# A hybrid decoder step on one core: k is projected first, q and k are turned inside v's projection, and the last stage issues all its gathers at once

## What is computed

```python
q_a = _rmsnorm(q_a.reshape(shp), q_norm_g[:, None, :])
k_a = _rmsnorm(k_a.reshape(shp), k_norm_g[:, None, :])
s = jnp.einsum('bnqrhe,bnkrhe->bnrhqk', qb, kk) * (E ** -0.5)
```

## Time and profile before

| | |
|---|---|
| median of three runs | 3180.73 us (3177.16 to 3184.13) |
| the profiled execution, its own time | 3173.9 us |
| its span, first to last instruction | 3172.2 us |
| attention stage, about 32 to 798 us | PE busy 96% from 32 to 790 us |
| combine stage, about 3120 us to the end | PE idle, DMA engines busy 69% from 3119 to 3172 us |

### The profile page before, as it was taken

The page is one execution under the profiler, slowest core; times in us unless marked ns, Lnnn a source line. Parts: engine busy times, 40 slices in busy tenths (PEclk is TensorE's granted clock), DMA queues, the critical chain, the costliest instruction groups (busy, mean ns, idle before and its releaser), DMA issues. The chain is left out here.

```text
span 3172.2 us, 33419 instructions
## 1 busy us (share of the span) xinstructions
PE 2852.2 (90%) x12984; PEld 1945.6 (61%) x12984; DVE 897.1 (28%) x1773; ACT 625.5 (20%) x1392; POOL 528.3 (17%) x543
## 2 busy tenths in 40 slices
PE   7999999999379999999999987999999499999992
PEld 4555776776157777777777776888855244444441
DVE  3222222222614334333433432212112411111113
ACT  2111112112013233332322332112000011111110
POOL 3122122222223122222312210000000000000002
PEclk9999999999669999999999969999999699999996
DMA  6002000200701011101100135662031399999994
GB/s 218 11 8 97 14 24 14 74 31 30 250 1 27 1 28 28 28 1 28 28 1 28 28 130 170 207 212 88 21 110 54 146 412 392 382 382 382 386 371 173
DMA packets 161553, 397.80 MB, mean 125 GB/s; under 512 B 10651, under 2 KB 102043, under 8 KB 149087
## 3 DMA queue, kind: packets, MB, share of 16 engines
q1 hardware_dynamic: 151662, 361.58, 31.2%
q0 software_dynamic: 6176, 21.83, 2.0%
q10 hardware_dynamic: 3584, 12.58, 1.0%
HBM read 323.01 MB, written 73.14 MB: 125 GB/s over the span
## 5 line engine op out<-in xcount | busy, mean ns | idle before, releaser
L440 PE MATMUL at_p<-ring,hT 128*128 128x512 f32 x1152 | 532.1, 610 | 1.6 <-PEq L2663 1.6
L981 PE MATMUL dn_p<-hT,ring 128*128 128x344 f32 x1536 | 483.7, 460 | 14.4 <-DVE dn_nq L1376 12.0
L440 PEld LDWEIGHTS at_p<-ring,hT 128*128 128x128 f32 x1152 | 304.2, 273 | 161.1 <-issue 80.8
L981 PEld LDWEIGHTS dn_p<-hT,ring 128*128 128x128 f32 x1536 | 282.3, 193 | 137.2 <-DVE dn_nq L1376 13.5
L1857 PE MATMUL mx_prod<-hT,ring 128*128 128x256 f32 (+1 forms) x1024 | 233.2, 381 | 3.0 <-PEq L2663 3.0
L1857 PEld LDWEIGHTS mx_prod<-hT,ring 128*128 128x128 f32 x1024 | 194.4, 190 | 31.1 <-issue 3.1
L2569 DVE TENSOR_TENSOR ex_hid<-ex_ps_u,ex_gated 128x512 f32<-128x512 f32 (+1 forms) x32 | 22.2, 693 | 507.5 <-PE ex_ps_u L2504 272.8
L1551 POOL TENSOR_TENSOR ring<-ring,dn_level 128x512 f32<-128x512 f32 x96 | 127.1, 1343 | 148.2 <-DVE ring L1395 80.3
L566 DVE COPY oBT<-at_p 128x256 f32<-128x256 f32 (+1 forms) x96 | 52.5, 547 | 299.6 <-PE at_p L490 299.5
L1533 POOL TENSOR_SCALAR ring<-ring,conv_w 128x1024 f32<-128x1024 f32 x24 | 72.0, 2998 | 363.0 <-ACT ring L1200 363.0
L1857 PE MATMUL mx_prod<-oBT,ring 128*128 128x256 f32 (+1 forms) x512 | 118.4, 385 | 12.0 <-DMA ring<-in_w_out_b 12.0
(11 more groups left out here) (427 smaller groups left out, 3953.9 us busy)
## 6 DMA issues: line engine op xcount, KB each, us to landing
ring<-in_w_e_gate SPq DMA_DIRECT2D x32, 2048.0 KB, 12.0
ring<-in_w_e_up SPq DMA_DIRECT2D x32, 2048.0 KB, 15.5
ring<-in_w_e_down SPq DMA_DIRECT2D x32, 2048.0 KB, 14.2
y_scratch<-tails SPq DMA_DIRECT2D x16, 2048.0 KB, 8.2
ring<-in_w_in SPq DMA_DIRECT2D x13, 2048.0 KB, 13.5
ring<-in_w_in SPq DMA_DIRECT2D x32, 512.0 KB, 6.6
ring<-in_cache_swa_kv SPq DMA_DIRECT2D x6, 2048.0 KB, 13.6
mx_w_a<-in_w_out_a SPq DMA_DIRECT2D x32, 256.0 KB, 2.9
```

Of the source, the lines that this page charges most:

```text
L440: mm = nc.tensor.matmul(bank, perm_tokens(m.hT, g, t, k), weights[:, k, :], start=(k == 0), stop=(k == KD - 1))
L981: mm = nc.tensor.matmul(bankp[j][:, 0:C3], weights[:, k, WPOS[part], :], m.hT[:, k, j * C3:(j + 1) * C3], start=(k == 0), stop=(k == KD - 1))
```

## The change

In the attention the projections go k, q, v, and v shares k's bank (`pv = pk`). `turn_qk` is split: `turn_k` stands after the 18th of the 24 matmuls, `turn_q` after the 22nd, and the last two matmuls and weigh 3 stand behind it. q is turned into a bank of its own, `tq`. q's weight is no longer multiplied in by POOL for prompt tiles: q is turned as it comes from the scaling (`sq`), where its weight belongs to a partition, and the copy to `qT` multiplies by the column `q_column` and by 1/8. ACT loads `q_column` with six small DMAs at the start of the stage. On DVE and ACT the steps for k and q change places, and the copy of kT stands before the scaling of q. The wait for v's copy moves from the scores to weigh 0. In the combine every tile has its own place in `ring`, POOL issues its 18 gathers without a wait, and the additions go in place into the residual `x1`, which is stored.

```diff
-                    for w, (name, bank) in enumerate((("q", pq), ("k", pk), ("v", pv))):
-                        if n >= 1 and name == "k":
-                            pe.wait_ge(S["k_scaled"], n)
+                    for name, bank in (("k", pk), ("q", pq), ("v", pv)):
+                        if n >= 1 and name == "q":
+                            pe.wait_ge(S["q_scaled"], n)
                         if name == "v":
-                            pe.wait_ge(S["q_scaled"], n + 1)
+                            pe.wait_ge(S["k_scaled"], n + 1)
...
-                def turn_qk(n):
+                def turn_k(n):
                     a = number[jobs[n]]
...
+                    pe.wait_ge(S["k_normed"], n + 1)
+                    if a >= 1:
+                        pe.wait_ge(S["probs_ready"], 8 * a)
...
+                def turn_q(n):
+                    pe.wait_ge(S["q_scaled"], n + 1)
+                    for hp in range(4):
+                        mm = nc.tensor.transpose(tq[:, hp * P:(hp + 1) * P], sq[:, 0, hp * P:(hp + 1) * P], m.ident)
+                    mm.then_inc(S["q_turned"], 1)
...
                         turn_probs(a, 2)
-                        fill(source, 5)
+                    else:
+                        fill(source, 18 if turns else 24)
+                    if turns:
+                        turn_k(jobs.index(nxt))
+                        fill(source, 4)
+                    if att:
                         weigh_values(a, 2)
                         turn_probs(a, 3)
-                        fill(source, 1)
+                    if turns:
+                        turn_q(jobs.index(nxt))
+                        fill(source, 2)
+                    if att:
                         weigh_values(a, 3)
-                    fill(source, 24)
-                    if nxt in number:
-                        turn_qk(jobs.index(nxt))
...
+                        if b == 0:
+                            dve.wait_ge(S["gain_landed"], 16 * 2 * NG)
+                        nc.vector.tensor_scalar(qT, tq.rearrange("p (h k) -> p h k", h=4),
+                                                m.q_column[:, nxt[0]:nxt[0] + 1], float(E) ** -0.5, ALU.mult, ALU.mult
+                                                ).then_inc(S["qT_ready"], 1)
...
+                for g in range(NG):
+                    for r in (0, E):
+                        act.dma_start(m.q_column[r:r + E, g:g + 1],
+                                      m.q_gain[:, g, :].rearrange("a (e c) -> (a e) c", c=1)).then_inc(S["gain_landed"], 16)
...
+                        if which == "q" and t < NT:
+                            continue
                         pool.wait_ge(S[which + "_scaled"], n + 1)
...
-                    if t >= 2:
-                        pool.wait_ge(both_added, t - 1)
                     for i in range(2):
-                        nc.gpsimd.indirect_dma_start(y[0:r, t % 2, i, :], None, m.y_scr,
+                    nc.gpsimd.indirect_dma_start(y[t][i][0:r], None, m.y_scr,
...
```

More of the change, by code:

```diff
@@ L526, in _ @@
                         pe.wait_ge(S["kT_ready"], a + 1)
-                        pe.wait_ge(S["v_copied"], jobs.index(att) + 1)
                         scores(a, 0)
                         scores(a, 1)
-                        fill(source, 24 if nxt and nxt[1] == NT else 6)
+                        fill(source, 6 if turns else 24)
                         turn_probs(a, 0)
@@ L622, in square @@
                     act.wait_ge(S[which + "_projected"], n + 1)
-                    if n >= 1:
-                        act.wait_ge(S[which + "_normed"], n)
+                    if which == "k" and n >= 1:
+                        act.wait_ge(S["k_normed"], n)
+                    elif n >= 1 and jobs[n - 1] in number:
+                        act.wait_ge(S["q_turned"], number[jobs[n - 1]] + 1)
+                    elif n >= 1:
+                        act.wait_ge(S["q_normed"], jobs[n - 1][0] + 1)
                     nc.scalar.activation(sq[banded(t, w), w, :], bank[banded(t, w), :], ACT.Square
@@ L669, in _ @@
                     r = rows(t)
-                    for w, which in enumerate("qk"):
+                    for which in "kq":
+                        w = "qk".index(which)
                         own = stat[banded(t, w), w]
@@ new lines, in stage_combine, with _ @@
+    rows = m.ring.rearrange("p a b -> p (a b)")
+    y = [[rows[:, (2 * t + i) * D:(2 * t + i + 1) * D] for i in range(2)] for t in range(NT + 1)]
+    first_added, both_added, stored = (semaphore(nc, m, "cb_" + n) for n in ("first_added", "both_added", "stored"))
+    y_landed = [semaphore(nc, m, f"cb_y_landed{t}") for t in range(NT + 1)]
+    with nc.Block() as block:
+        @block.gpsimd
+        def _(pool):
+            for t, r in TILES:
+                for i in range(2):
+                    nc.gpsimd.indirect_dma_start(y[t][i][0:r], None, m.y_scr,
+                                                 bass.IndirectOffsetOnAxis(m.dest_u[0:r, i, t:t + 1], 0)
+                                                 ).then_inc(y_landed[t], 16)
+        @block.vector
+        def _(dve):
+            for t, r in TILES:
+                x1 = m.x1[t][0:r]
+                dve.wait_ge(y_landed[t], 32)
+                nc.vector.scalar_tensor_tensor(x1, y[t][0][0:r], m.row_w[0:r, 0, t:t + 1], x1, ALU.mult, ALU.add
+                                               ).then_inc(first_added, 1)
+                dve.wait_ge(first_added, t + 1)
+                nc.vector.scalar_tensor_tensor(x1, y[t][1][0:r], m.row_w[0:r, 1, t:t + 1], x1, ALU.mult, ALU.add
+                                               ).then_inc(both_added, 1)
+        @block.sync
+        def _(sp):
+            for t, r in TILES:
+                sp.wait_ge(both_added, t + 1)
+                dst = m.y_prompt[t * P:(t + 1) * P, :] if t < NT else m.y_sample
+                sp.dma_start(dst, m.x1[t][0:r]).then_inc(stored, 16)
+            sp.wait_ge(stored, 16 * (NT + 1))
```

93 lines of the change are left out of this document (26 added, 67 removed).

## The result

The changed kernel takes 3140.43 us (median of four executions, 3138.79 to 3146.40), the kernel before beside it 3179.75 us; the ratio is 0.9878, with a 95% interval from 0.9861 to 0.9896. That is 39 us or 1.2% less, where 29.5 us were forecast. Executions of one kernel differ by up to 14 us here, and much of that lies in stages that the change does not touch (from the last weigh of the attention to the first gather of the combine they take 2323.0 us in some traces and up to 2335.1 in others), so what follows compares stage by stage.

The account below looks back on a forecast made before the run. PE, idle before each attention step's scores, and the DMA engines in the combine were taken as bounds. Attention -26, start +3.5, combine -7 sum to -29.5; from the median 3180.7 that gives 3151 us (chance 0.55), range 3140 to 3164.

Parts of the forecast that it names:

- The seams: Attention: 24 waits before a step's scores vanish, 1.14 us each, 27.4 less 1.4 for broken matmul rows: -26 us.
- The cover it worked out for qT's copy: Attention: transposes, two matmuls and weigh 3 give 2.56 us where 1.45 is needed, 1.1 us more.
- the low end of 0.69 to 1.38: Attention: assumed length in us of the new two-factor copy to qT; 0.69 taken, twice that the high end.
- The start: Start of attention: the first projection now needs k's chunk, which is loaded second and lands at 35.8 us: +3.5 us, once.
- The combine: Combine: gathers no longer wait for additions, so the eighth tile lands at 3157.0 us and the end is 3165.3: -7 us.
- I take 350: 28.0 us: Combine: 9.8 MB left after 3129 us flow at 350 GB/s, chosen between 336 and 367, taking 28.0 us.
- the rival in which stores give way to gathers: Combine: gathers go ahead of stores, so it gains 11 us instead of 7; 3147 us, chance 0.10.
- The additions do hold up issues: Combine rival: ten gather issues each wait for an addition of 1.28 us; gain 4 us instead of 7; 3154 us, chance 0.18.
- Half the seams: Attention rival: qT's two-factor copy takes 2.4 us, scores wait 0.6 per seam, 14 us of gain lost; 3165 us, chance 0.11.
- the waiting turn_q: Attention rival: q's chain 4 us longer, PE waits 2.7 us for q's scaling in 24 steps; 3216 us; slower, chance 0.06.
- the 1.3 us of slack: Attention: PE has 6.4 us of work from the 16th matmul to turn_q, against 5.1 until q's scaling ends.
- the allowance for scatter and for the share of stores: Lower end of the range: 3147 less 3.5 us scatter, 1.4 for the seam's upper end, 2 for unknown stores' share: 3140.

Follow-up runs that it names:

- the three copies: Changed kernel with three more copies of the turned q on VectorE ahead of the one to qT; first projection to last weigh 750.1 us, 12.0 more.
- The attention alone: Attention part of the change with the combine of the kernel before; 3158.24 us, ratio 0.9932.
- two tiles ahead: Changed kernel in which a tile's gathers wait for the additions of the tile two before; combine 58.4 us against 40.5.
- the run with one input: Changed kernel with the combine's 18 additions each replaced by a sum over one gathered row block into 8 columns; combine 40.2 us against 40.5.
- four tiles ahead: Changed kernel in which a tile's gathers wait for the additions of the tile four before; combine 40.4 us against 40.5.
- the shorter ends: Changed kernel with k loaded first, the 8-row tile gathered mid-combine, first additions awaiting only their own gather, last addition and store halved; 3135.46 us, ratio 0.9859.
- side-by-side run: The shorter ends, unaltered, on the same chip as the changed kernel; 3139.79 us (ratio 0.9868) against 3139.99 us (0.9882).

## Why the prediction was right or wrong

**The seams: right.** -27.0 us against -26. All that it named showed: no idle time before the scores, none on the transposes, a step of group 2 shorter by 1.15 us (1.1 to 1.14 forecast). The cover it worked out for qT's copy, 1.1 us, is 1.18 in the row and 1.3 by the three copies. The copy took 0.75 us, near the low end of 0.69 to 1.38 that was chosen.

**The start: right.** +3.1 against +3.5, released by the DMA; and the run with k loaded first gives 3.5 back.

**The combine: the mechanism right, its size wrong.** The step that failed is the term "I take 350: 28.0 us". The bytes were right: the stretches of the combine add up to 2.1 MB in the first 8.45 us and to 11.7 MB by 3128.86 us, 8.5 of gathers and 3.2 of stores (3.4 forecast), so 9.6 MB were left where 9.8 were forecast. They took 23.8 us, which is 403 GB/s. Of the stretches from which 336 and 367 were read, the one from 3157 runs into the end of a burst (DMA share 0.93). The one from 3145 does not, its share is 1.00 throughout, but it holds the slow beginning of a burst: 326 GB/s in its first 2 us, with full engines, and 395 in the last 3. In that part the trace of before had this row, which I averaged away:

```profile
3148.00:3150.00 2.00, 0.00 (x0) 0.00 (x0) 1.61 (x2) 0.00 (x0) 0.00 (x0) 0.50 1.00 395
```

The attention alone, with this same combine, reached 418 and 406 GB/s late in a burst (3120 to 3124 us). So two things went into the forecast's rate that the change takes away, gaps and slow beginnings. With the waits of two tiles ahead the bursts come back, with four they do not; why full engines move less at the start of a burst stays open.

The combine came out at the -11 of the rival in which stores give way to gathers, but not for its reason: the stores did not give way, the rate was higher.

**The rivals.** The additions do hold up issues, but each only for about the rest of the addition that it meets and not for the 1.28 us that the rival charged ten times: the sixteenth gather is issued 20.8 us after the first, against 18.7 in the run with one input, 2.1 us in all instead of 12.8. POOL is done 7 us before the eighth tile's addition, so it costs nothing. Half the seams and the waiting turn_q did not come about: turn_q starts 2.7 us after the end of q's scaling (585.52), more than the 1.3 us of slack that were worked out.

**The sum.** On the profiled executions -35.1 against -29.5: 4.2 of the 5.6 us are the combine, 1.0 the seams, 0.4 the start. The other 5 us between 3151 and 3140 are 1.0 by which the median of the kernel before came out lower beside the changed kernel, and 4.2 between the medians and the profiled executions. The time lies 0.4 us above the lower end of the range, because no case in the range had a flow over 367 GB/s; that it is inside is owed to the allowance for scatter and for the share of stores, which is luck.

## What to carry to other kernels

Read a transfer rate from a stretch in which the engines are full and the burst is well under way, a couple of microseconds if need be; a mean over a burst holds its gap and its slow beginning, which the change takes away. An operation whose result is waited for at a stage's seam can go ahead of the last independent work, and the price of getting that wrong is read off by making it longer until the wait shows. When two inputs change their order of use, their loads must change with it: here that was the one loss of the change that the stages show, 3.5 us.

## What the runs showed of the hardware

With the DMA engines full (share 1.00 to 1.03), indirect gathers of 4 KB rows moved 338 to 380 GB/s over stretches of 6 or 7 us and 413 over one of 4 us; stores alone moved 404; both at once 407 to 421 in the changed kernel and with four tiles ahead, and 380 in one stretch of the shorter ends (3109 to 3114 us, side-by-side run). An issue of a gather on POOL takes 0.94 us when nothing meets it. One that begins while an addition with two inputs in SBUF runs on DVE ends 0.74 to 0.83 us after that addition in the changed kernel, and lasts up to 1.80 us there and 1.94 with two tiles ahead; beside a sum with one input it lasts 0.87 to 0.94 us.
